# Hybrid decoder layer, one core: query and key made with tokens on partitions and normed along the free axis, two products given to GpSimd

## What is computed

```python
proj = rms_norm(x, norm1_g) @ w_in            # RWKV | q k v | pool | gates
# RWKV-7 mixer, 8 heads x 64: p mixed with the token before
r, k, v = p[..., :W], p[..., W:2*W], p[..., 2*W:3*W]
kk = normalise(k * k_k)                       # per head
k  = k * (1 + (a - 1) * k_a)
S_t = S * w_t + (S a_t) b_t + v_t k_t ;  o_t = S_t r_t      # scan over time
bonus = sum(r * k * r_k, per head) * v
# attention, 8 heads x 64
q = rms_norm(q, qn_g); k = rms_norm(k, kn_g)  # per token and head, over 64 channels
y = softmax(q k^T / 8 - slope * dist, causal) v
```

## Time and profile before

| | |
|---|---|
| median of 3 runs | 517.11 us (516.94 to 517.74) |
| the profiled execution | 516.5 us, of which its span is 514.7 us |
| TensorE matmul busy | 502.2 us, 98% of the span, granted clock 1.000 |
| VectorE busy | 304.1 us, 59% |
| ScalarE busy | 249.6 us, 48% |
| GpSimd busy | 47.3 us, 9% |
| chain that ended last | TensorE 92%, VectorE 4% |
| from HBM | 75.2 MB, 148 GB/s over the span |

### The profile page before, as it was taken

The page is one execution under the profiler, slowest core; times in us unless marked ns, Lnnn a source line. Parts: engine busy times, 40 slices in busy tenths (PEclk is TensorE's granted clock), DMA queues, the critical chain, the costliest instruction groups (busy, mean ns, idle before and its releaser), DMA issues.

```text
span 514.7 us, 9588 instructions
## 1 busy us (share of the span) xinstructions
PE 502.2 (98%) x4064; PEld 458.3 (89%) x4064; DVE 304.1 (59%) x423; ACT 249.6 (48%) x379; POOL 47.3 (9%) x48
## 2 busy tenths in 40 slices
PE   3999999999999999999999999999999999999997
PEld 3989988988889878899999998899999999999995
DVE  4667897444453796436426986676555555555542
ACT  5677442555663235655424334564444454444440
POOL 1002003220570030000001220000000000000000
PEclk9999999999999999999999999999999999999999
DMA  9876452433422223344315646558666665666612
GB/s 256 264 213 190 135 168 83 124 100 106 125 82 83 74 70 105 113 115 124 120 46 165 194 138 204 161 166 223 196 193 187 185 196 171 193 188 193 199 46 82
DMA packets 101660, 76.87 MB, mean 149 GB/s; under 512 B 2545, under 2 KB 93297, under 8 KB 101618
## 3 DMA queue, kind: packets, MB, share of 16 engines
q1 hardware_dynamic: 101618, 76.26, 50.2%
HBM read 75.20 MB, written 1.05 MB: 148 GB/s over the span
## 4 chain that ended last, share of the span: by engine, by line
PE 92%; DVE 4%; DMA 1%; ACT 1%; issue 1%; SPq 0%; ACTq 0%
PE bank L460 26%; PE bank L461 24%; PE bank L462 24%; PE bank L667 2%; PE bank L685 2%; DMA stage<-in_w_in 1%; PE bank L696 1%; PE bank L553 1%; PE bank L774 1%; DVE mat L1141 1%; PE bank L731 1%; PE bank L720 1%; PE bank L712 1%; PE bank L730 1%; PE bank L634 1%
## 5 line engine op out<-in xcount | busy, mean ns | idle before, releaser
L1031 DVE TENSOR_TENSOR w_lo<-stage,w_hi 128x1024 fp32r<-128x1024 f32 x138 | 172.3, 1253 | 127.2 <-ACT w_hi L812 127.1
L812 ACT CAST w_hi<-stage 128x1024 fp32r<-128x1024 f32 x138 | 143.9, 1049 | 111.6 <-PE bank L462 83.9
L460 PE MATMUL bank<-h_hi,w_hi 128*128 128x256 f32 x656 | 192.5, 293 | 1.1 <-DVE h_lo L1055 0.8
L461 PE MATMUL bank<-h_lo,w_hi 128*128 128x256 f32 x656 | 185.7, 283 | 0.0
L462 PE MATMUL bank<-h_hi,w_lo 128*128 128x256 f32 x656 | 185.6, 283 | 0.0
L460 PEld LDWEIGHTS bank<-h_hi,w_hi 128*128 128x128 f32 x656 | 125.5, 191 | 10.1 <-issue 7.1
L461 PEld LDWEIGHTS bank<-h_lo,w_hi 128*128 128x128 f32 x656 | 125.7, 192 | 0.6
L462 PEld LDWEIGHTS bank<-h_hi,w_lo 128*128 128x128 f32 x656 | 125.6, 192 | 0.0
L460 PE MATMUL bank<-w_hi,r_hi 128*128 128x512 f32 x128 | 50.1, 391 | 0.0
L461 PE MATMUL bank<-w_lo,r_hi 128*128 128x512 f32 x128 | 50.1, 391 | 0.0
L462 PE MATMUL bank<-w_hi,r_lo 128*128 128x512 f32 x128 | 49.9, 390 | 0.0
(11 more groups left out here) (208 smaller groups left out, 632.8 us busy)
## 6 DMA issues: line engine op xcount, KB each, us to landing
stage<-in_w_ff SPq DMA_DIRECT2D x64, 512.0 KB, 4.2
stage<-in_w_in SPq DMA_DIRECT2D x54, 512.0 KB, 3.9
stage<-in_w_branch SPq DMA_DIRECT2D x12, 512.0 KB, 3.5
stage<-in_w_out SPq DMA_DIRECT2D x8, 512.0 KB, 3.4
xs<-in_x SPq DMA_DIRECT2D x2, 512.0 KB, 4.4
out<-xs SPq DMA_DIRECT2D x4, 256.0 KB, 2.1
cst<-in_consts SPq DMA_DIRECT2D x1, 897.0 KB, 7.4
lora<-in_g_up SPq DMA_DIRECT2D x1, 256.0 KB
```

The source lines that it names most:

```text
L460: pe.matmul(o, lh, rh, start=first, stop=False)
L461: pe.matmul(o, lh, rl, start=False, stop=False)
L812: nc.scalar.copy(w_hi[:, v % RING], stage[:, v % STAGES]).then_inc(hi_done, 1)
L1031: dve.tensor_tensor(w_lo[:, v % RING], stage[:, v % STAGES], w_hi[:, v % RING].bitcast(F32), ALU.subtract)\
```

## The change

Units 7 to 10 become `tok` units like v's: q in 7 and 8 (banks 1 and 0), k in 9 and 10 (banks 3 and 2). ScalarE only squares them (from PSUM), VectorE sums each head's 64 squares along the free axis, GpSimd takes the root twice per tensor (128x8 each), VectorE multiplies the bank by the root, and TensorE transposes the normed tiles: eight at (10, 1) for q, eight at (12, 1) for k. ScalarE moves them to `qraw`/`kraw` with the norm's gain. The `ss` matmuls are gone. On GpSimd, between `inverse_root(kk_tok)` and `add_identity(0, 0)`, stand now the two products that VectorE had at (5, 2) and the bonus operand that it had at (7, 0), as four `tensor_scalar` and one 128x1024 `tensor_tensor`.

```diff
-UNITS += [("feat", N_RWKV + c) for c in (0, 256, W, W + 256)]
-UNITS += [("tok", N_RWKV + 2 * W, kh) for kh in range(2)]
+UNITS += [("tok", N_RWKV + c, kh) for c in (0, W, 2 * W) for kh in range(2)]
...
+S_TURN = (10, 12)
...
                 elif u[0] == "tok" and u[2] == 0:
-                    use(("tok", u[1], 0), 1)
-                    use(("tok", u[1], 1), 0, dense=True)
+                    b = 2 if u[1] == N_RWKV + W else 0
+                    use(("tok", u[1], 0), b + 1)
+                    use(("tok", u[1], 1), b, dense=True)
...
# TensorE
-                if S_QK < t <= S_QK + 4 and p == 3:
-                    n = t - 1 - S_QK
-                    copied(pe, ("unit", t - 1))
-                    o = room(pe, ("ss", n))
-                    for c in range(TT):
-                        for jj in range(2):
-                            ins = pe.matmul(o[:, 4 * c + 2 * jj:4 * c + 2 * jj + 2],
-                                            sq_att[n % 2][:, T * jj + P * c:T * jj + P * c + P],
-                                            cst[:, C_BLK:C_BLK + P:HD], start=True, stop=True)
-                    ins.then_inc(full_of(("ss", n)), 1)
...
+                if t in S_TURN and p == 1:
+                    n = S_TURN.index(t)
+                    for tt in range(TT):
+                        copied(pe, ("tok", N_RWKV + W * n, tt))
+                        o = room(pe, ("qb", n, tt))
+                        for j in range(PAIRS):
+                            ins = pe.transpose(o[:, P * j:P * j + P], sq_att[tt][:, P * j:P * j + P], ident)
+                        ins.then_inc(full_of(("qb", n, tt)), 1)
# ScalarE
+                if t in S_TURN and p == 1:
+                    n = S_TURN.index(t)
+                    for tt in range(TT):
+                        o = take(act, ("qb", n, tt))
+                        nc.scalar.mul((qraw, kraw)[n][:, :, P * tt:P * tt + P], q4(o[:]), gq8 if n == 0 else col(V_KN))\
+                          .then_inc(drained_of(("qb", n, tt)), 1)
...
+                elif t in (S_QK + 1, S_QK + 3):
+                    for tt in range(TT):
+                        o = take(act, ("tok", u[1], tt))
+                        nc.scalar.activation(sq_att[tt], o[:], ACT.Square).then_inc(qk_sq, 1)
# VectorE
-                if (t, p) == (5, 2):
...
-                        dve.tensor_tensor(ar[c][:, :, 1], rmix[:, :, P * c:P * c + P], e_up[:, c, :, 1:129], ALU.mult)
...
-                    for j in range(PAIRS):
-                        ins = dve.scalar_tensor_tensor(out=ksq[:, j], in0=rmix[:, j], scalar=col(V_RK + j), in1=k2[:, j],
-                                                       op0=ALU.mult, op1=ALU.mult)
-                    ins.then_inc(rk_ready, 1)
...
+                if t + 1 in S_TURN and p in (2, 3):
+                    n = S_TURN.index(t + 1)
+                    for tt in range(TT):
+                        if p == 2:
+                            dve.wait_ge(qk_sq, 2 * n + tt + 1)
+                            link(dve.tensor_reduce(qk_tok[tt], by_head(sq_att[tt]), AX_X, ALU.add))
+                            dve.tensor_scalar(qk_tok[tt], qk_tok[tt], 1.0 / HD, RMS_EPS, ALU.mult, ALU.add).then_inc(qk_ms, 1)
+                        else:
+                            dve.wait_ge(qk_inv, 2 * n + tt + 1)
+                            name = ("tok", N_RWKV + W * n, tt)
+                            o = take(dve, name)
+                            dve.tensor_tensor(by_head(sq_att[tt]), by_head(o[:]),
+                                              qk_tok[tt].unsqueeze(2).to_broadcast([P, HEADS, HD]), ALU.mult)\
+                               .then_inc(drained_of(name), 1)
# GpSimd, after inverse_root(kk_tok, kk_inv)
+            for u in (3, 4):
+                copied(pool, ("unit", u))
+            for c in range(TT):
+                for i in range(2):
+                    copied(pool, ("cum", c, i))
+                pool.tensor_tensor(ar[c][:, :, 1], rmix[:, :, P * c:P * c + P], e_up[:, c, :, 1:129], ALU.mult)\
+                    .then_inc(r_ready, 1)
+            for i in range(2):
+                copied(pool, ("kb", i))
+            for j in range(PAIRS):
+                pool.tensor_scalar(ksq[:, j], rmix[:, j], col(V_RK + j), None, ALU.mult).then_inc(rk_part, 1)
+            pool.wait_ge(rk_part, PAIRS)
+            pool.wait_ge(k2_ready, 1)
+            pool.tensor_tensor(ksq, ksq, k2, ALU.mult).then_inc(rk_ready, 1)
```

More of the change, by code:

```diff
@@ L166, in pe_uses @@
         out += [(("bonus", 0),), (("bonus", 1),)]
-    if S_QK < t <= S_QK + 4 and p == 3:
-        out.append((("ss", t - 1 - S_QK), 2))
-    if S_QK + 1 < t <= S_QK + 5 and p == 1:
-        out.append((("qb", t - 2 - S_QK), 3))
+    if t in S_TURN and p == 1:
+        out += [(("qb", S_TURN.index(t), tt),) for tt in range(TT)]
     if product_place(t, p):
@@ L311, in build_layer @@
         kk_tok = small[:, 56:72].rearrange("p (c h) -> p c h", c=TT)
-        qk_tok = [small[:, 72 + 8 * i:80 + 8 * i].rearrange("p (c h) -> p c h", c=TT) for i in range(2)]
+        qk_tok = [small[:, 72 + 8 * i:80 + 8 * i] for i in range(2)]
+        by_head = lambda ap: ap.rearrange("p (h v) -> p h v", h=HEADS)
         kkb = flat[:, 3072:4096].rearrange("p (c n) -> p c n", c=TT)
@@ L374, in build_layer @@
         lora_ready = sem("lora_ready")
-        kkraw_ready, ksq_ready, kk_inv, qk_inv, kkb_ready, qkb_ready = (
-            sem(n) for n in ("kkraw_ready", "ksq_ready", "kk_inv", "qk_inv", "kkb_ready", "qkb_ready"))
+        kkraw_ready, ksq_ready, kk_inv, kkb_ready = (sem(n) for n in ("kkraw_ready", "ksq_ready", "kk_inv", "kkb_ready"))
+        qk_sq, qk_ms, qk_inv = (sem(n) for n in ("qk_sq", "qk_ms", "qk_inv"))
         own = sem("own")
-        rk_ready, ops_ready = sem("rk_ready"), sem("ops_ready")
+        k2_ready, rk_part, rk_ready, ops_ready, r_ready = (
+            sem(n) for n in ("k2_ready", "rk_part", "rk_ready", "ops_ready", "r_ready"))
         nt_ready, x1_ready, xte_ready = (
@@ L545, in products @@
                     pe.wait_ge(ops_ready, 1)
+                    pe.wait_ge(r_ready, c + 1)
                 for e in range(2):
@@ L760, in extra @@
                     if p == 1 and h < HEADS:
-                        copied(pe, ("qb", 3))
+                        copied(pe, ("qb", 1, 0))
+                        copied(pe, ("qb", 1, 1))
                         j, rows = h // 2, slice(HD * (h % 2), HD * (h % 2) + HD)
@@ L961, in finish @@
                           .then_inc(keep_part, 1)
[L962 to L970, removed]
+                elif t in (S_QK + 1, S_QK + 3):
+                    for tt in range(TT):
+                        o = take(act, ("tok", u[1], tt))
+                        nc.scalar.activation(sq_att[tt], o[:], ACT.Square).then_inc(qk_sq, 1)
+                elif t == S_VA + 1:
                     for tt in range(TT):
@@ L1077, in extra @@
                     link(ins)
-                    dve.tensor_tensor(k2, k2, kmix, ALU.mult)
+                    dve.tensor_tensor(k2, k2, kmix, ALU.mult).then_inc(k2_ready, 1)
                 if (t, p) == (5, 0):
@@ L1117, in extra @@
                                           vmix[:, 2 * i:2 * i + 2], ALU.mult).then_inc(drained_of(("bonus", i)), 1)
[L1118 to L1129, removed]
                 if product_place(t, p):
@@ L1360, in inverse_norm @@
             def inverse_norm(n):
-                copied(pool, ("ss", n))
-                inverse_root(qk_tok[n % 2], qk_inv)
+                for tt in range(TT):
+                    pool.wait_ge(qk_ms, 2 * n + tt + 1)
+                    inverse_root(qk_tok[tt], qk_inv)
             add_identity(0, 0)
-            inverse_norm(0)
             add_identity(0, 1)
-            for n in (1, 2, 3):
+            for n in range(2):
                 inverse_norm(n)
```

10 lines of the change are left out of this document (removed).

## The result

| | before | the change |
|---|---|---|
| median | 516.94 us (516.54 to 517.74, 5 runs) | 520.3 us (518.74 to 521.15, 5 runs) |
| ratio to before | | 1.0063, 95% interval 1.0042 to 1.0084 |
| profiled execution | 516.5 us, span 514.7 | 521.15 us, span 519.4 |
| mean granted TensorE clock | 1.000 | 0.993 |

A forecast was written before the change was run, and what follows sets the result against it. TensorE, busy without a gap from 57 us on, was taken to bound the kernel. Terms -4.2 + 3.0 + 0.8 + 0.1 = -0.3 us on the profiled 516.5, plus 0.6 to the median, gave 516.8 us; range 515.6 to 519.2.

The forecast's parts named there:

- the hold-up: Before `finish(6)`: GpSimd's new work delays VectorE, and so TensorE, by 0.8 us, bounds 0 and 3.1.
- TensorE gains 4.2 us: Units 7 to 10: no `ss` matmuls (3.5 us) and cheaper dense work (0.7 us), all on the path.
- A new wait at (7, 1): TensorE waits 2.86 us for bank 0 until VectorE's `finish(6)` empties it; +3.0 us with restart.
- `a_s` (L1076) would not be held: On VectorE before `finish(6)`: GpSimd's new work would not delay this operation.
- the fourth `tensor_scalar` holds the `low` up: Before `finish(6)`: GpSimd's last `tensor_scalar`, from 60.1 to 61.0 us, delays VectorE's next `low` by 0.8 us.
- the big product "waits until `finish(6)`": GpSimd's 128x1024 product stays pending while VectorE's operations overlap in issue, delaying none; 2.3 us more if it gets in.
- the pair at 84.38: Sign in the earlier trace: GpSimd's 128x512, issued at 84.38, took 2.74 us; VectorE's `low`, issued at 84.76, went first.
- Nothing on the clock: The forecast sum held no term for TensorE's clock behind the new wait at (7, 1).
- The chain at (9, 1) to (10, 1): From q's last product through norm and roots to its transposes: TensorE loses 0.1 us, bounds 0 and 0.6.
- Rival 1: Behind L1087, before `finish(6)`: the big product gets in, GpSimd's hold-up is 2.9 us; 518.9 us, chance 0.30.

The follow-up runs named there:

- e3: The change with the banks of q, k and v exchanged and GpSimd's new work given back to VectorE; 512.76 us, ratio 0.9909.
- e2: The change with all of GpSimd's new work given back to VectorE, banks as in the change; 516.66 us, ratio 0.9984.
- e8: The change with GpSimd's 128x1024 product made to wait until `finish(6)` is over; 517.56 us, ratio 0.9995.
- e9: The change with six one-column memsets on GpSimd ahead of its 128x1024 product, to issue it later; 519.76 us, ratio 1.0052.
- e11: The change with twenty one-column memsets on GpSimd ahead of its 128x1024 product, to issue it later; 520.46 us, ratio 1.0055.
- e5: The change with forty needless 128x256 matmuls on TensorE ahead of part (7, 1); 517.99 us, ratio 1.0016.
- e10: The change with the banks of q, k and v exchanged and GpSimd's 128x1024 product held back until `finish(6)`; 512.88 us, ratio 0.991.
- e4: The kernel before with GpSimd's new work alone, q, k and banks as before; 518.04 us, ratio 1.001.
- e1: The change with banks exchanged: q and v in 3 and 2, k in 1 and 0; 514.81 us, ratio 0.9947.
- e7: The change with only the two receptance products on GpSimd, the bonus operand back on VectorE at (7, 0); 516.32 us, ratio 0.9988.
- e6: The change with `finish(6)` put ahead of the last three operand products on VectorE; 517.73 us, ratio 1.0011.

## Why the prediction was wrong

Two of its terms were wrong, and neither alone explains the miss. With the hold-up at its measured 2.4 us in place of 0.8, the prediction's own sum is -4.2 + 3.0 + 2.4 + 0.1 = +1.3, that is 518.4 us and inside its range. The clock, which stands in no term, carried the time out of it.

- *TensorE gains 4.2 us.* Right: 4.3 in the account, 4.4 between the same two points in e3, and 4.9 in its median (3.9 to 5.5 by the interval of the ratio).
- *A new wait at (7, 1), 2.86 us by VectorE's queue, not shortened by what (5, 2) gives away.* Right: 2.87 in e2.
- *The hold-up by GpSimd is 0.8 us.* **This step failed**: it was 2.4, which made the wait 5.3 us. The prediction had three parts in it. That `a_s` (L1076) would not be held: right, 1.21 us. That the fourth `tensor_scalar` holds the `low` up by 0.8: it was 0.16 us (1.38 against 1.22). Its row ends at 61.71, 0.8 us into the row of `low`, so by these rows (GpSimd's are rough) the two did not exclude each other for the whole of it; in e8 the fourth `tensor_scalar` ends at 64.30, and L1083, issued at 63.51, lost 0.2 us by it and no more. That the big product "waits until `finish(6)`", as VectorE's operations overlap in issue: it went in at once and held one operand product for 2.2 us. The rule was drawn from one pair of rows, 84.38 and 84.76, and the first-come order, which the prediction set aside for it, is what the change, e9 and e11 show. The Trainium skill, page "SBUF — State Buffer", section "Who interferes with whom", says: "Issue order, not op shape, decides who blocks." With 61.79 against 62.25 us in the change and 62.61 against 63.10 in e11 the trace agrees. That the first one holds the pair "for the whole instruction", as the prediction quotes, agrees with the 2.2 us of the product and not with the 0.16 of the `tensor_scalar`. For the pair at 84.38 it does not, and that stays open: GpSimd's operation there had just been released from an idle wait, and one can think that it asks for the port later than its row begins. No run tried that.
- *Nothing on the clock.* **A term was missing, put at nothing without a reason.** A wait was added to a TensorE that had none, and the matmuls behind it were priced at the upper level. They ran at the lower one: 2.9 us in the profiled execution, 2.3 to 2.8 by e5, 2.1 by the sum above. All windows read before the run had a clock of 1.00, and none of them held a wait of over half a microsecond.
- *The chain at (9, 1) to (10, 1), 0.1 us.* Right within its bounds: 0.2 us, in the change and in e3.
- *The rivals.* Rival 1 (518.9 us, chance 0.30) has the right mechanism for the port, by another path: the product went in not at the gap behind L1087 but into the gap-free row behind `low`. It priced the hold-up at 2.9 where 2.4 was measured, and it lacks the clock too. The range should have reached over its time by what an idle TensorE may cost.

There was a sign of the clock in the trace of before, behind the long wait at its start. Sixteen transposes take 3.65 us there, where eight of the same shape take 1.04 later:

```profile
7.45 3.65 PE L538 MATMUL bank<-cst,big 128*128 128x128 f32 x16 [7.45 <-DVE big L1043]
...
51.76 1.04 PE L602 MATMUL bank<-cst,mat 128*128 128x128 f32 x8
```

The next matmul behind the eight starts at 52.56, so one of them costs 0.10 us, and one of the sixteen about 0.2. That is the pace of the lower level, though the clock column shows 1.00 at the start. That it is the clock is argued from the pace alone; no run tested it.

## What to carry over

Before you change which PSUM bank an early dense unit uses, list who must have drained it, and read in the trace when that drain ends, not when it could: a late drain that nobody waits for is invisible in every list of waits. An offload to GpSimd is not free for VectorE while VectorE runs a row of operations with two SBUF operands (2.4 us here); put it behind the drain that others need, as e10 did. And price a wait of a TensorE that had none as its length plus what the clock may cost behind it.

## What was unexpected of the hardware

How often the clock falls after a wait grows with the wait: in some executions at about three microseconds, in all 14 at five. Executions whose mean granted clock was 0.997 or less, by TensorE's longest new wait in the one profile of each kernel (where in the launch it fell is known only for the profiled ones):

```
longest wait   kernels                      executions with the clock down
none or 0.3    before (65), e3, e5, e10     0 of 81
0.8            e4                           0 of 10
1.1            e1                           1 of 5
2.7 to 2.9     e7, e2                       9 of 20
3.1 to 3.3     e8, e6                       14 of 20
5.1            the change, e9, e11          14 of 14
```

The Trainium skill, page "TensorE: Matmul & The Clock Gate", says that the clock follows how busy the engine has been recently and knows two levels; in these rows it is 0.50 or 1.00 once settled.

It need not fall in the wait. In the profile of e8 the three matmuls behind the wait of 3.1 us (68.77 on) still have the upper pace, and from 69.80 to 73.20 they start 0.43 us apart, a loss of 1.5 us. And the mean does not tell all: the slow start of the launch in the profile of the change, or in that of e1 (mean 1.000), is not in it.

The second: the profile may put a real wait down to "issue". In e1 and e4 the 1.1 and 0.8 us ahead of L622 are so labelled, although VectorE's `finish(6)` ended 0.1 us before the matmul in both.
